# Order of the first product tile, order of the first attention's helpers, and the row pitch of the transposed activations

## Time and profile before

| | us |
|---|---|
| median of 3 runs (lowest, highest) | 832.33 (832.21, 832.71) |
| the profiled execution, device time | 832.52 |
| its span in the profile | 830.8 |
| PE busy | 818.2 (98%) |
| PEld busy | 649.5 (78%) |
| DVE busy | 513.4 (62%) |
| ACT busy | 456.7 (55%) |

### The profile page before, as it was taken

The page is one execution under the profiler, slowest core; times in us unless marked ns, Lnnn a source line. Parts: engine busy times, 40 slices in busy tenths (PEclk is TensorE's granted clock), DMA queues, the critical chain, the costliest instruction groups (busy, mean ns, idle before and its releaser), DMA issues.

```text
span 830.8 us, 11698 instructions
## 1 busy us (share of the span) xinstructions
PE 818.2 (98%) x4452; PEld 649.5 (78%) x4452; DVE 513.4 (62%) x1075; ACT 456.7 (55%) x879; POOL 36.5 (4%) x95
## 2 busy tenths in 40 slices
PE   8999999999999999999999999999999999999996
PEld 7877666788888888888877878777878888888885
DVE  5856869786545555586465565565568765555544
ACT  7846877764444344475565555555657544344431
POOL 1000004800000000000000000000000000000000
PEclk9999999999999999999999999999999999999998
DMA  9955311165664466568544435352524665456501
GB/s 320 315 196 183 96 52 52 49 228 171 217 217 159 151 199 214 161 215 274 172 159 144 161 116 189 106 199 102 160 95 155 192 212 177 152 186 217 204 1 50
DMA packets 108904, 137.49 MB, mean 165 GB/s; under 512 B 6273, under 2 KB 92337, under 8 KB 108721
## 3 DMA queue, kind: packets, MB, share of 16 engines
q1 hardware_dynamic: 107760, 132.53, 48.3%
q0 software_dynamic: 992, 4.19, 1.4%
q10 hardware_dynamic: 96, 0.02, 0.0%
HBM read 134.64 MB, written 2.10 MB: 165 GB/s over the span
## 4 chain that ended last, share of the span: by engine, by line
PE 94%; DVE 4%; ACT 1%; issue 1%; POOL 0%; ACTq 0%; POOLq 0%; DVEq 0%
PE ps L1685 84%; PE ps L1694 7%; PE ps L1935 1%; PE ps L1908 1%; DVE w_lo L1138 1%; PE ps L1746 0%; ACT xt_hi L646 0%; PE ps L1947 0%; DVE xt_lo L1186 0%; DVE probs L1331 0%; ACT junk L658 0%; DVE h L1456 0%; DVE h L1462 0%; DVE tmp L1460 0%; DVE probs L1357 0%
## 5 line engine op out<-in xcount | busy, mean ns | idle before, releaser
L1138 DVE TENSOR_TENSOR w_lo<-w_raw,w_hi 128x1024 fp32r<-128x1024 f32 x240 | 287.7, 1223 | 93.7 <-ACT w_hi L637 91.2
L1685 PE MATMUL ps<-w_hi,xt_hi 128*128 128x512 f32 x760 | 311.6, 410 | 1.2 <-DVE w_lo L1138 0.8
L1685 PE MATMUL ps<-w_lo,xt_hi 128*128 128x512 f32 x760 | 299.4, 394 | 0.0
L1685 PE MATMUL ps<-w_hi,xt_lo 128*128 128x512 f32 x760 | 298.9, 393 | 0.0
L637 ACT ACTIVATE w_hi<-w_raw 128x1024 fp32r<-128x1024 f32 x240 | 246.2, 1059 | 0.0
L1685 PEld LDWEIGHTS ps<-w_hi,xt_hi 128*128 128x128 f32 x760 | 143.8, 189 | 37.5 <-issue 9.2
L1685 PEld LDWEIGHTS ps<-w_hi,xt_lo 128*128 128x128 f32 x760 | 143.3, 189 | 32.3
L1685 PEld LDWEIGHTS ps<-w_lo,xt_hi 128*128 128x128 f32 x760 | 143.9, 189 | 25.5
L909 ACT ACTIVATE st_hi<-ps 128x256 fp32r<-128x256 f32 x40 | 15.4, 385 | 119.4 <-PE ps L1694 119.4
L1474 DVE TENSOR_TENSOR st_lo<-ps,st_hi 128x256 fp32r<-128x256 f32 x40 | 17.0, 425 | 78.1 <-ACT st_hi L909 77.9
L1685 PE MATMUL ps<-w_hi,st_hi 128*128 128x512 f32 x160 | 63.2, 395 | 0.0
(11 more groups left out here) (244 smaller groups left out, 802.2 us busy)
## 6 DMA issues: line engine op xcount, KB each, us to landing
w_raw<-in_ffn_w_gu SPq DMA_DIRECT2D x88, 512.0 KB, 5.0
w_raw<-in_dil_w_in SPq DMA_DIRECT2D x72, 512.0 KB, 4.6
w_raw<-in_ffn_w_down SPq DMA_DIRECT2D x44, 512.0 KB, 4.7
w_raw<-in_nsa_w_in SPq DMA_DIRECT2D x20, 512.0 KB, 7.6
w_raw<-in_nsa_w_o SPq DMA_DIRECT2D x8, 512.0 KB, 4.9
w_raw<-in_dil_w_o SPq DMA_DIRECT2D x8, 512.0 KB, 4.3
w_k<-in_nsa_cmp_wk SPq DMA_DIRECT2D x2, 1024.0 KB, 7.9
w_raw<-in_nsa_cmp_wv SPq DMA_DIRECT2D x2, 1024.0 KB, 11.1
```

Source lines behind the costliest of these rows:

```text
L1138: dve.tensor_tensor(w_lo[:, n.slot, c:c + 1024], w_raw[:, n.slot, c:c + 1024], w_hi[:, n.slot, c:c + 1024].bitcast(F32), ALU.subtract)\
L1685: ins = pe.matmul(o, s, m, start=start, stop=stop, **kw)
```

## The change

1. The first product tile gets its own order on PE (`first_gemm`). In each half it takes the high x high products as soon as `w_hi` is there, then low x high, and the products with `w_lo` last; it waits for the four semaphores separately. The idle transposes ahead of it go from 22 to 15. ACT writes the high parts of rows 128 to 255 ahead of its first row sum instead of behind it; DVE writes their low parts right behind `split(1)`, and the angles go behind `split(3)` and the gate weights. `h_rs` and the halves of `split(2)` alternate.
2. In the first attention ACT evacuates tile 8 and serves `attend(5)` before the second half of piece 12 and all of piece 13; DVE weights pair 4 before it splits piece 12, and takes the rotation, the mask of pair 6, the low part of the output and the weighting of pair 5 before the rest of pieces 12 and 13.
3. `xt_hi` and `xt_lo` get rows of 256 numbers (1024 bytes). The dilated layer reads and writes the same memory under the names `xd_hi` and `xd_lo`, at the old pitch.

```diff
-        xt_hi = sb("xt_hi", [P, KT, XT_PITCH], F32R)
-        xt_lo = sb("xt_lo", [P, KT, XT_PITCH], F32R)
+        at_xt = [zone(KT * XT_PITCH * 4) for k in range(2)]
+        xt_hi, xt_lo = (sb(f"xt_{k}", [P, KT, S], F32R, at=at) for k, at in zip(("hi", "lo"), at_xt))
+        xd_hi, xd_lo = (sb(f"xd_{k}", [P, KT, XT_PITCH], F32R, at=at) for k, at in zip(("hi", "lo"), at_xt))
...
@@ ACT, start
             split(1)
+            xt_out(0, 1, 0, 0)
+            xt_out(0, 1, 1, 0)
             act.wait_ge(x_loaded[0], 16)
             h_squares(0, 0)
-            xt_out(0, 1, 0, 0)
-            xt_out(0, 1, 1, 0)
@@ ACT, first attention
             attend(4)
-            split(12, (1,))
-            split(13, (0,))
             proj_evac(q_rows)
             attend(5, between=lambda: cmp_turned(0))
-            split(13, (1,))
+            split(12, (1,))
             ot_hi_nsa(0)
+            split(13, (0,))
             attend(6)
             turn_q(1, 0, 3, 2)
+            split(13, (1,))
             attend(7)
@@ DVE, start (the angles, lines 1198 to 1215, move from behind split(1) to behind gw_lo)
             split(1)
+            xt_lo_out(0, 1, 0, 0)
+            xt_lo_out(0, 1, 1, 0)
+            dve.wait_ge(rows_t, 2)
+            dve.tensor_copy(g_t[:, 16:48], bank(2, 16, 32)).then_inc(gt_ready, 1)
+            h_rs(0, 0)
+            split(2, (0,))
+            h_rs(0, 1)
+            split(2, (1,))
...
+            split(3)
+            dve.wait_ge(gw_hi_ready, 1)
+            dve.tensor_tensor(gw_lo[:, :, :], gw_raw[:, :, :], gw_hi[:, :, :].bitcast(F32), ALU.subtract)\
+               .then_inc(gw_ready, 1)
             dve.wait_ge(pos_loaded, 16)
             dve.wait_ge(rope_ready, 1)
...
@@ DVE, first attention
             mask_pair_nsa(5)
+            norm_nsa(4)
             split(12, (0,))
+            rope(0, 9, stage_rot, 0, 8, 0)
+            mask_pair_nsa(6)
+            ot_lo_nsa(0)
+            norm_nsa(5)
             split(12, (1,))
             split(13, (0,))
-            rope(0, 9, stage_rot, 0, 8, 0)
-            norm_nsa(4)
-            ot_lo_nsa(0)
-            mask_pair_nsa(6)
-            split(13, (1,))
-            norm_nsa(5)
             mask_pair_nsa(7)
             norm_nsa(6)
+            split(13, (1,))
             mask_pair_nsa(8)
@@ PE
-            idle_turns(22)
+            idle_turns(15)
...
-            nsa_gemm(0, N_CMPKV, mid=turn_rest)
+            def first_gemm():
+                def product(kt, stat, mov, start=False, stop=False):
+                    p, c = Piece(N_CMPKV + kt // 4), kt % 4 * 512
+                    return mm(bank(0), stat[:, kt, 0:P], mov[:, p.slot, c:c + 512], start, stop)
+
+                for half in range(2):
+                    p = Piece(N_CMPKV + half)
+                    if half:
+                        turn_rest()
+                    pe.wait_ge(xt_hi_ready[0], half + 1)
+                    for u0 in (0, 2):
+                        pe.wait_ge(hi_ready, p.halves(u0 // 2 + 1))
+                        for kt in (4 * half + u0, 4 * half + u0 + 1):
+                            product(kt, xt_hi, w_hi, start=kt == 0)
+                        if u0 == 0:
+                            pe.wait_ge(xt_ready[0], half + 1)
+                        for kt in (4 * half + u0, 4 * half + u0 + 1):
+                            product(kt, xt_lo, w_hi)
+                    for u0 in (0, 2):
+                        pe.wait_ge(lo_ready, p.halves(u0 // 2 + 1))
+                        for kt in (4 * half + u0, 4 * half + u0 + 1):
+                            ins = product(kt, xt_hi, w_lo, stop=kt == KT - 1)
+                ins.then_inc(proj_done[0], 1)
+
+            first_gemm()
             nsa_gemm(1, N_CMPKV)
```

More of the change, by code:

```diff
@@ L644, in xt_out @@
                     kt = 4 * half + k
-                    src, dst = xt_views(b, m, half, kt, xt_hi)
+                    src, dst = xt_views(b, m, half, kt, xd_hi if b == 2 else xt_hi)
                     ins = act.activation(dst, src, ACT.Copy, scale=g_t[:, 8 * gain + kt:8 * gain + kt + 1])
@@ L1183, in xt_lo_out @@
                     kt = 4 * half + k
-                    src, dst = xt_views(b, m, half, kt, xt_lo)
-                    _, hi = xt_views(b, m, half, kt, xt_hi)
+                    src, dst = xt_views(b, m, half, kt, xd_lo if b == 2 else xt_lo)
+                    _, hi = xt_views(b, m, half, kt, xd_hi if b == 2 else xt_hi)
                     ins = dve.scalar_tensor_tensor(dst, src, g_t[:, 8 * gain + kt:8 * gain + kt + 1],
@@ L1197, in _, with rope @@
             split(1)
+            xt_lo_out(0, 1, 0, 0)
[6 more added lines that the diff above has]
+            split(2, (1,))
+            def rope(i, e, stage, m, heads, table):
+                a, b = rope_a[:, 0:heads, :], rope_b[:, 0:heads, :]
+                x16 = view(stage, m * 512, [[DH, heads], [1, ROT]])
+                x1 = view(stage, m * 512, [[DH, heads], [1, 8]])
+                x2 = view(stage, m * 512 + 8, [[DH, heads], [1, 8]])
+                dve.wait_ge(proj_out[i], e)
+                dve.tensor_tensor(a, x16, view(cos2, table * ROT, [[0, heads], [1, ROT]]), ALU.mult)
+                dve.tensor_tensor(rope_b[:, 0:heads, 0:8], x2, view(sin2, table * ROT, [[0, heads], [1, 8]]),
+                                  ALU.mult)
+                link(dve.tensor_tensor(rope_b[:, 0:heads, 8:16], x1,
+                                       view(sin2, table * ROT + 8, [[0, heads], [1, 8]]), ALU.mult))
+                dve.tensor_tensor(x16, a, b, ALU.add).then_inc(roped[i], 1)
+                dve.wait_ge(roped[i], e - 2)
+            split(3)
+            dve.wait_ge(gw_hi_ready, 1)
+            dve.tensor_tensor(gw_lo[:, :, :], gw_raw[:, :, :], gw_hi[:, :, :].bitcast(F32), ALU.subtract)\
+               .then_inc(gw_ready, 1)
             dve.wait_ge(pos_loaded, 16)
@@ L1215, in _ @@
                .then_inc(angles_ready, 1)
[L1216 to L1225, removed]
-                x16 = view(stage, m * 512, [[DH, heads], [1, ROT]])
-                x1 = view(stage, m * 512, [[DH, heads], [1, 8]])
-                x2 = view(stage, m * 512 + 8, [[DH, heads], [1, 8]])
-                dve.wait_ge(proj_out[i], e)
-                dve.tensor_tensor(a, x16, view(cos2, table * ROT, [[0, heads], [1, ROT]]), ALU.mult)
-                dve.tensor_tensor(rope_b[:, 0:heads, 0:8], x2, view(sin2, table * ROT, [[0, heads], [1, 8]]),
-                                  ALU.mult)
-                link(dve.tensor_tensor(rope_b[:, 0:heads, 8:16], x1,
-                                       view(sin2, table * ROT + 8, [[0, heads], [1, 8]]), ALU.mult))
-                dve.tensor_tensor(x16, a, b, ALU.add).then_inc(roped[i], 1)
-                dve.wait_ge(roped[i], e - 2)
-            split(3)
-            dve.wait_ge(gw_hi_ready, 1)
-            dve.tensor_tensor(gw_lo[:, :, :], gw_raw[:, :, :], gw_hi[:, :, :].bitcast(F32), ALU.subtract)\
-               .then_inc(gw_ready, 1)
             split(4)
@@ L1527, in ffn @@
                     dve.wait_ge(xt_ready[2], 2)
-                    dve.tensor_copy(xt_hi[:, :, S:S + 2], xt_hi[:, :, 0:2])
-                    dve.tensor_copy(xt_lo[:, :, S:S + 2], xt_lo[:, :, 0:2]).then_inc(xt_padded, 1)
+                    dve.tensor_copy(xd_hi[:, :, S:S + 2], xd_hi[:, :, 0:2])
+                    dve.tensor_copy(xd_lo[:, :, S:S + 2], xd_lo[:, :, 0:2]).then_inc(xt_padded, 1)
             norm_nsa(15)
@@ L1705, in three, with gemm @@
                 return mm(o, s_lo, m_hi, False, stop)
-            def gemm(b, m, pc, first, last, done=None, mid=None, need=None, cols=None, half_done=None):
+            def gemm(b, m, pc, first, last, done=None, mid=None, need=None, cols=None, half_done=None,
+                     hi=xt_hi, lo=xt_lo):
                 for half in range(2):
@@ L1722, in gemm @@
                         at = cols or slice(m * P, (m + 1) * P)
-                        ins = three(bank(b), xt_hi[:, kt, at], xt_lo[:, kt, at],
+                        ins = three(bank(b), hi[:, kt, at], lo[:, kt, at],
                                     w_hi[:, p.slot, c:c + 512], w_lo[:, p.slot, c:c + 512],
@@ L2232, in dil_gemm @@
                      cols={QK: None, V01: slice(x.m, S, 2), V2: slice(x.m + 2, S + 2, 2)}[x.kind],
-                     need=need, mid=mid)
+                     need=need, mid=mid, hi=xd_hi, lo=xd_lo)
             def dil_turn(x):
```

## The result

The changed kernel takes 823.38 us (median of 4 runs, 823.15 to 823.58) against 832.27 us (4 runs, 832.03 to 832.71): ratio 0.9893, 95% interval 0.9875 to 0.991. It is 8.9 us faster; the forecast was 3.9 us, with the range ending at 825.3. Both reorderings did what was forecast, and the pitch, which was put at nothing, brought the rest.

A forecast was written before the change was run, and what follows sets the result against it. PE was taken as the bound (busy 98% of the span, 94% of the last chain). 832.5 - 1.9 (start) - 2.0 (attention) + 0 (pitch) = 828.6, as a median 828.4 us; range 825.3 to 830.4.

The forecast's parts named there:

- Part 1: First tile at the start: second tile begins at 15.9 instead of 17.82, -1.9 us, bounds -1.9 and -0.6.
- ACT's 3.28 us of air: ACT's wait before the evacuation at 39.41: 3.28 - 1.9 - 1.2 leaves 0.1 us.
- the chain of the angles: DVE's angle steps near the start, put at 1.9 us and ending at 28.1.
- Part 2: First attention: two waits of PE, 0.78 and 1.23 us, vanish; -2.0 us, bounds -2.0 and -0.8.
- Part 3: Pitch of xt_hi and xt_lo outside the dilated layer: no effect, 0 us, bounds -4.2 and +4.2.
- the bound of -4.2: Pitch's best case: 3 ns less on each of 1416 products from xt, reaching the speed of st_hi.
- The control: Products from ot_hi_s, which has the new pitch, at 393 ns against 394 for xt_hi; basis for taking 0.
- (a): Rival for the pitch: short rows are faster by 1.5 to 3 ns a product, 826.3 to 824.2 us; chance 0.17.
- (b): Rival for the start: its gain is eaten by ACT behind the angles, +1.3, 829.7 us; chance 0.09.
- (c): Rival for the first attention: it only passes its wait on, +1.2, 829.6 us; chance 0.10.
- (d): Rival for both reorderings: PE waits for something else that was hidden, about 831.5 us; chance 0.05.
- (e): Rival for the pitch: 1024-byte rows make PE's two reads meet, slower; 835.5 us at 5 ns a product; chance 0.06.

The follow-up runs named there:

- e1: Changed kernel with xt_hi and xt_lo back at rows of 1088 bytes, so both reorderings without the new pitch: 828.99 us, ratio 0.9957.
- e3: Kernel before with only the start's changes (first tile's order, 15 idle turns, ACT and DVE orders beside it): 830.53 us, ratio 0.9977.
- e8: Changed kernel with xt_hi and xt_lo 256 bytes further on, rows of 1024 bytes kept: 823.14 us, ratio 0.9890.
- e12: The changed kernel itself, run again unaltered: 823.63 us, ratio 0.9894 to the kernel before.
- e2: Kernel before with only the pitch change, xt_hi and xt_lo at rows of 1024 bytes outside the dilated layer: 827.23 us, ratio 0.9935.
- e4: Kernel before with only the first attention's new order on ACT and DVE: 830.64 us, ratio 0.9977.
- e5: Changed kernel with xt_hi and xt_lo 64 bytes further on, rows of 1024 bytes kept: 831.24 us, ratio 0.9985.
- e7: Changed kernel with xt_hi and xt_lo 128 bytes further on, rows of 1024 bytes kept: 829.33 us, ratio 0.9962.
- e10: Changed kernel with xt_lo alone 64 bytes further on, xt_hi in its place: 826.57 us, ratio 0.9933.
- e9: Changed kernel with w_hi, w_lo and w_raw 64 bytes further on and everything else 256 bytes further on: 826.35 us, ratio 0.9928.
- e6: Changed kernel with every tile in SBUF 64 bytes further on: 823.50 us, ratio 0.9894.

## Why the prediction was wrong

**Part 1 was right, a little low.** The first half ends near 11.7 and the second tile starts at 15.77 (forecast 15.9). What stands ahead of it on that axis comes up to 0.35 us early, and not because inputs landed earlier: the first turns of x start at 5.80 (5.85 before) and take 1.09 us in the place of 1.39. The trace's clock record has the full clock (2.4 GHz) from 5.6 us on, before the change from 6.5. In the runs with the new start that moment lies anywhere from 4.4 to 7.6 us, and the first product starts at 8.2 to 9.3, the earlier the earlier the clock. The stretch by stretch account held as well: `w_lo` came in time, ACT's 3.28 us of air were used to the last, and nothing was given back. By itself the start brought 2.1 us (1.9 forecast).

Two steps behind it were wrong, and that they did no harm is luck. I put ACT's table load behind the wait for the angles, and it runs at 25.66, ahead of it, which gives ACT 1.3 us. And the chain of the angles took 3.4 us (25.49 to 28.93) and not 1.9: one TENSOR_SCALAR on DVE took 1.58 us for 0.17, and ended when POOL's clearing of `tb` did (27.48 and 27.46). POOL had waited for `gw_lo`, behind which the change puts the angles. `e1`, `e3`, `e8` and `e12` show the same 1.57 to 1.58 us beside the same clearing; in `e2` and `e4`, with the old order, it is 0.17. The two errors cancel. (The terms for the angles' end also add up to 27.9, not 28.1.)

**Part 2 was right in size and mechanism.** Alone 2.0 us. The weighting of pair 4 comes 2.5 us before PE wants it (2.2 forecast). The moved halves run into no one: DVE idles 0.15 us before mask 7, for scores that PE has yet to finish, and PE waits for none of its work.

**Part 3 is the step that failed: the pitch was put at 0 and brought 5.4 us.** It was beyond the bound of -4.2 too, and by what the bound left out: the products from `xt`, to which it applied, gained 4.0 us, and those from `st_hi` and `st_lo`, counted at nothing, 1.1 (`e2`, product by product). Three readings led there.

- The control was a poor one. `ot_hi_s` has the new pitch and was not faster (393 against 394 ns). But its products run in stretches of three to nine between turns and scores, and their distance is 231 ns after the change as well, though `ot_hi_s` and `ot_lo_s` are in place in both kernels (201856 and 208000, again 128 modulo 256). The 24 products from `xt` in the same stretches did change their pitch and gained nothing either (`e2`). Such stretches could not have shown a gain.
- The bound was read from a neighbour that paid as well. `st_hi` stood between the blocks of `xt` and ran at 229.2 ns; with `xt` in its place it runs at 226.7. In `e5`, `e7` and `e10` it is slowed again without being moved. The true floor stood in the kernel before: products 20 to 27 behind a turn (the end of the down block and block 0 of the next tile, which starts at offset 0) took 226 to 229 ns, while in blocks 1 to 3 the distances were 228 to 236, 232 in the mean. One stretch, with block 0 and the first of block 1:

```profile
219.08 0.39 PE L1685 MATMUL ps<-w_hi,xt_hi 128*128 128x512 f32 x1
219.31 0.39 PE L1685 MATMUL ps<-w_lo,xt_hi 128*128 128x512 f32 x1
219.54 0.39 PE L1685 MATMUL ps<-w_hi,xt_lo 128*128 128x512 f32 x1
219.76 0.40 PE L1685 MATMUL ps<-w_hi,xt_hi 128*128 128x512 f32 x1
220.00 0.39 PE L1685 MATMUL ps<-w_lo,xt_hi 128*128 128x512 f32 x1
```

- The view was the wrong one. A mean by operand hides the floor, whether of the durations, which are modelled (394, 391), or of the distances (231.1, 229.2); only distances by position show it. 1416 products at 4.4 ns, from 231.1 to that floor of 226.7, would have been a bound of -6.2 us, plus 1.2 for `st_hi`.

The list of products in the prediction adds up to 1440, not 1416. The 24 for the gates don't belong in it: they read `xt` as the moving operand, 256 columns wide. The total is right for the wide products without them.

The Trainium skill was weighed here ("SBUF — State Buffer", "Who interferes with whom": PE has a read port for each operand and waits for nobody). It speaks of engines against each other, and I let it speak of PE's two reads against one another: exactly 0. The runs differ from that reading: 9 ns for one product of three by 64 bytes of address (`e10`).

**The rivals.** (a), with 0.17, had the right sign and not the reason: short rows as such are not faster (`e5`), rows that all lie in place are. Its price held for the 1416 products (1.5 to 3 ns; they gained 4.0 us, 2.8 ns each) and left out `st_hi` and `st_lo`, with 1.1 us. (b), (c) and (d) did not occur. (e) looked at the right thing with the wrong sign: the places of the two operands against each other do count, but products are slow when they are *not* alike modulo 256 bytes. With its chance of 0.06 it should have led to a chance for the opposite sign larger than 0.17, since the kernel before was the one with mixed places. The forecast was right in direction; a range down to 822 would have held it.

## What to carry to other kernels

Where thousands of equal products bound a kernel, read the distances of their starts by position in the sequence, not the mean duration by operand: groups at 226 and at 232 ns in one loop are a few us that no wait shows. A padded pitch for one stage needn't be paid by the others, since two names on the same memory cost nothing. And before "this operand has that layout and isn't faster" is taken as evidence, check that it runs in stretches long enough to be fast.

## What the runs showed of the hardware

- A float32r product of 128 x 128 by 128 x 512 starts 226.7 ns after the one before when the stationary block starts at the same place modulo 256 bytes as the moving one. With all `xt` blocks 64 bytes on it is 233.5 ns, 128 bytes on 232.2, and with the weights 64 bytes on (blocks 192 on) 229.4 (`e5`, `e7`, `e9`); with everything moved alike (`e6`) or by 256 (`e8`) it stays at 226.7 to 227.8. Shifts other than 64, 128, 192 and 256 bytes were not tried. That it is the two operands' reads that meet is the simplest reading of this; the runs show the relation of the places, not the cause.
- Products next to a block that is out of place are slower too: those from `st_hi` by 0.8 to 1.5 ns (`e7`, `e5`) and by 2.5 in the kernel before. In the kernel before and in `e5` the first six to eight of the twelve carry it, and the next ones are at 226.7.
- Behind a turn the second to the sixth product take 228 to 236 ns though they are in place, and 227 from the seventh on (the changed kernel's networks).
- A table load of ACT runs ahead of the wait that stands in front of its ACTIVATE: 25.66 against a sine at 28.97.
- A TENSOR_SCALAR of 128 x 16 on DVE took 1.58 us in the place of 0.17 while POOL cleared 128 x 2048 numbers, and ended with it (27.48 and 27.46). The DVE steps just before it, a CAST and a TENSOR_TENSOR, took 0.16 and 0.18; the second of them ran inside the clearing.
